# Cross attention of the samples: score and value products take the four sequences of a half in turn

## What is computed

```python
def _cross_attend(h, mk, mv, p):
    n, t = h.shape[:2]                                  # samples: n = 8, t = 4
    q = (h @ p['w_xq']).reshape(n, t, XA_HEADS, XA_HEAD_DIM)
    logits = jnp.einsum('nthd,nmhd->nhtm', q, mk).astype(jnp.float32) * XA_HEAD_DIM ** -0.5
    pr = jax.nn.softmax(logits, axis=-1).astype(mv.dtype)
    o = jnp.einsum('nhtm,nmhd->nthd', pr, mv).reshape(n, t, D_MODEL)
    return o @ p['w_xo']
```

## Time and profile before

| | |
|---|---|
| median of 3 runs | 1905.02 us (1904.67 to 1906.63) |
| profiled execution's own time | 1907.62 us |
| its span, first to last instruction | 1905.6 us |
| PE busy | 1817.0 us, 95% |
| DVE busy | 925.2 us, 49% |
| ACT busy | 530.8 us, 28% |
| mean granted TensorE clock | 0.979 |
| `cross_sample`, first score pass to first pass of the next block | 953.6 to 1009.5 us |

### The profile page before, as it was taken

One profiled execution on the slowest core, in us unless ns is written; L12 is line 12 of the kernel. 1 busy time (PEld: TensorE's weight loads), 2 busy tenths in 40 slices (PEclk: granted clock), 3 DMA queues, 4 the chain that ended last, 5 costly groups with the idle time before them and its releaser, 6 DMA issues. The chain is left out here.

```text
span 1905.6 us, 28207 instructions
## 1 busy us (share of the span) xinstructions
PE 1817.0 (95%) x11818; PEld 1613.5 (85%) x11818; DVE 925.2 (49%) x1881; ACT 530.8 (28%) x1089; POOL 249.9 (13%) x110
## 2 busy tenths in 40 slices
PE   8999988589999899999989999999999999999997
PEld 6889977357767769998935679999999999999997
DVE  6422130467787754433411336545544545455547
ACT  7421000258888522201301212111102101111121
POOL 0011200000000000000000104223224213313320
PEclk9999999789999999999999999999999999999999
DMA  5122657611120341113070012011011101101102
GB/s 192 39 87 56 189 156 195 192 67 57 57 80 14 114 147 50 34 45 133 1 309 22 0 39 77 4 64 67 23 45 67 37 31 67 56 12 67 56 16 91
DMA packets 98306, 145.57 MB, mean 76 GB/s; under 512 B 40637, under 2 KB 73597, under 8 KB 96541
## 3 DMA queue, kind: packets, MB, share of 16 engines
q1 hardware_dynamic: 94094, 140.62, 22.1%
q10 hardware_dynamic: 4088, 3.17, 0.6%
HBM read 132.69 MB, written 14.19 MB: 77 GB/s over the span
## 5 line engine op out<-in xcount | busy, mean ns | idle before, releaser
L1928 PE MATMUL ps<-ff_in_high,ff_weights_low 128*128 128x352 f32 x1056 | 342.6, 324 | 0.0
L1928 PE MATMUL ps<-ff_in_high,ff_weights_high 128*128 128x352 f32 x1056 | 340.2, 322 | 0.0
L1928 PE MATMUL ps<-ff_in_low,ff_weights_high 128*128 128x352 f32 x1056 | 338.0, 320 | 0.0
L1928 PEld LDWEIGHTS ps<-ff_in_high,ff_weights_high 128*128 128x128 f32 x1056 | 198.8, 188 | 0.3
L1928 PEld LDWEIGHTS ps<-ff_in_low,ff_weights_high 128*128 128x128 f32 x1056 | 198.3, 188 | 0.2
L1928 PEld LDWEIGHTS ps<-ff_in_high,ff_weights_low 128*128 128x128 f32 x1056 | 198.1, 188 | 0.0
L2132 DVE TENSOR_TENSOR x<-ps,x 128x352 f32<-128x352 f32 x216 | 113.3, 525 | 134.5 <-PE ps L1946 134.5
L1897 POOL TENSOR_TENSOR ff_weights_low<-ff_weights,ff_weights_high 128x1024 fp32r<-128x1024 f32 x44 | 106.0, 2409 | 456.3 <-ACT ff_weights_high L2028 456.3
L1946 PE MATMUL ps<-ff_act_high,ff_down_high 128*128 128x352 f32 (+1 forms) x496 | 158.3, 319 | 0.2
L1946 PE MATMUL ps<-ff_act_high,ff_down_low 128*128 128x352 f32 (+1 forms) x496 | 156.6, 316 | 0.0
L1946 PE MATMUL ps<-ff_act_low,ff_down_high 128*128 128x352 f32 (+1 forms) x496 | 156.5, 316 | 0.0
(11 more groups left out here) (335 smaller groups left out, 3508.3 us busy)
## 6 DMA issues: line engine op xcount, KB each, us to landing
ff_weights<-in_w_up SPq DMA_DIRECT2D x22, 512.0 KB, 4.5
ff_weights<-in_w_gate SPq DMA_DIRECT2D x22, 512.0 KB, 4.4
ff_down<-in_w_down SPq DMA_DIRECT2D x22, 512.0 KB, 3.5
top<-in_mem_v SPq DMA_DIRECT2D x8, 1024.0 KB, 16.5
top<-in_mem_kt SPq DMA_DIRECT2D x6, 1024.0 KB, 10.1
x<-in_xt SPq DMA_DIRECT2D x3, 1408.0 KB, 10.1
x<-in_pool_cmp SPq DMA_DIRECT2D x32, 128.0 KB, 3.1
big<-in_pool_cmp SPq DMA_DIRECT2D x32, 128.0 KB, 2.7
```

The costliest lines, as they stand in the source:

```text
L1928: last = nc.tensor.matmul(K.bank[3 * s + x][:, 0:b - a], wt[:, s, ws], h[:, k, a:b], start=k + n == 0, stop=k == KD - 1 and n == 2)
```

## The change

Both loops of products are turned inside out, for scores and for values: the sequence `x` is now the innermost loop. The scores run over the eight pieces `c` and in each over the four sequences; the values over the output bank `b` and the piece `m`, and in each over the four sequences. Number, shapes, operands and sums of the products stay. The waits for keys and for values stand in the first round of four (each ahead of its sequence's first product), and the semaphores `k_used` and `pv` are raised in the last round, once for each sequence.

```diff
-                for x in range(4):
-                    n = 4 * half + x
-                    pe.wait_ge(k_came[n], 16)
-                    for c in range(KD):
+                for c in range(KD):
+                    for x in range(4):
+                        n = 4 * half + x
+                        if c == 0:
+                            pe.wait_ge(k_came[n], 16)
                         last = nc.tensor.matmul(K.bank[0][32 * x:32 * x + 32, 0:MEM], qbd[:, c, n, :], kr[n][:, c, :],
                                                 start=c == 0, stop=c == KD - 1)
-                    last.then_inc(k_used, 1)
+                        if c == KD - 1:
+                            last.then_inc(k_used, 1)
...
-                for x in range(4):
-                    n = 4 * half + x
-                    pe.wait_ge(v_came[n], 16)
-                    for b in range(2):
-                        for m in range(2):
+                for b in range(2):
+                    for m in range(2):
+                        for x in range(4):
+                            n = 4 * half + x
+                            if b + m == 0:
+                                pe.wait_ge(v_came[n], 16)
                             last = nc.tensor.matmul(K.bank[2 + b][32 * x:32 * x + 32, :], pt[:, m, 32 * x:32 * x + 32],
                                                     vr[n][:, m, b * 512:(b + 1) * 512], start=m == 0, stop=m == 1)
-                    last.then_inc(pv, 1)
+                            if b + m == 2:
+                                last.then_inc(pv, 1)
```

## The result

| | before | after |
|---|---|---|
| median, four runs each | 1905.18 us (1904.67 to 1906.63) | 1887.61 us (1883.85 to 1890.65) |
| ratio | | 0.9906, 95% interval 0.9883 to 0.9928 |
| span of the profiled execution | 1905.6 us | 1881.8 us |
| `cross_sample`, first score pass to first pass of the next block | 55.9 us | 36.3 us |

The account below looks back on a forecast made before the run. PE's one stream of matmuls was taken to bound the kernel. Faster batches save 26.2 us, 8.5 us of it become waits for loads, so 17.7 us off the 1905.0 us median gives 1887.3 us; range 1883.0 to 1892.0 us.

Parts of the forecast that it names:

- A round of four costs one pass: Score and value products: four strips in turn take one pass's time, 0.216 us at 256 columns; scores 3.6 us a half.
- The landing of values 7 sets the end: Second half's values: ready by 979.1 us but waiting for values 7 until 982.8 us; next block at 991.8 us.
- The waits: PE in `cross_sample`: waits of 2.4 us for values 3, 2.4 us for keys 7, 3.7 us for values 7.
- The values' size: Value batch of each half: 5.3 us instead of 10.53 us; 3.6 us at full clock, 7.0 us at 1.2 GHz throughout.
- The sum: Whole stage: 26.2 us saved on PE, 8.5 us become waits for loads, next block 17.7 us earlier.
- rival 1: Loads in `cross_sample` bind less: 1883.6 us, 1881.9 us with full clock too, 1878.8 us if none mattered; chance 0.12.

Follow-up runs that it names:

- half-load kernel: Changed kernel with half of every load of cached keys and values left out, products as many and as long: 1874.55 us, ratio 0.9820 to before.
- second series: The changed kernel run once more, unaltered, beside the kernel before: 1884.15 us, ratio 0.9889; its profile shows a stage of 38.2 us.
- early keys: Changed kernel with the loads of keys 4, 6 and 7 issued in the block before: 1882.71 us, ratio 0.9883 to the kernel before.

## Why the prediction was right

- **A round of four costs one pass**: right. 3.66 us for 64 passes, 3.6 us forecast, for the width of 256 columns that no row of before had shown. The rule of the Trainium skill, "TensorE: Matmul & The Clock Gate", Part 3, that weight loads overlap only across row groups, is not what this shows: the 64 weight loads of 0.11 us, 7 us of them, lie within the same 3.66 us.
- **The landing of values 7 sets the end**: right, and the step that mattered. It was put at 29.2 us after the stage's start and came at 28.9 us, though issued 5.4 us earlier relative to that start. Reckoned by PE alone, the forecast would have been 1878.8 us, outside the interval of what was measured.
- **The waits**: the three that were named are the three in the trace. Values 3 came a little earlier (8.6 us after the stage's start instead of 8.9), keys 7 too (18.6 instead of 19.0 us). No wait for `w_xo` appeared: its first piece landed 6 us ahead of the next block. How long each landing keeps a ready batch, forecast as 2.4, 2.4 and 3.7 us (8.5 us), came out as 2.0, 1.1 and 3.7 us (6.8 us) in the first profile and 1.9, 4.0 and 2.2 us (8.1 us) in the second, where keys 6 were late too. The parts move with the clock of the batch ahead; only the last landing, which none of them moves, sets the end.
- **The values' size**: mis-sized. 10.53 to 5.3 us was forecast, 5.2 us less, with the half clock as it stood in the trace of before. At full clock the batch takes 3.6 us, and which of the two occurs changes from profile to profile. The two ends were given as bounds; the value chosen, 5.3 us, came about true for the last batch in one of two profiles (5.53 us for its 26 passes; 3.62 us in the other). With no landing waited for, the stage lost 29.1 us, not 26.2, because the value batches of before met the half clock and those of the half-load kernel did not.
- **The sum** of 17.7 us met the median of 17.6 us partly by luck: the second series of the changed kernel is 22.1 us under the kernel before beside it (1884.15 and 1906.22 us), a value that the prediction had for rival 1, and the start of the stage alone scatters by 5 us. What is sure is the stage: 38.2 us forecast, 36.3 and 38.2 us found. The 38.2 us are met to the tenth only because a landing 0.3 us early and a batch 0.2 us longer cancel. The forecast also left the next block's start at half clock; both profiles of the changed kernel start it at full clock, 1.7 us more of gain.

## What to carry to other kernels

When matmuls fill only a strip of the array's columns, put those of different strips next to each other in the program, innermost; it costs no instruction, and here it brought 11.47 us of scores to 6.27 us with two strips in turn and to 3.66 us with four. Before counting the gain, list the landing of every load that the slow batch had hidden: PE meets the latest of a group at its first round, and here the last landing plus the last batch was the new length of the stage. Then move those loads forward: early values 2 and 3 and keys 4 took 8 to 10 us more off the stage. Judge such a stage by its own length in the trace, since the rest of a long program can scatter by as much as the gain in question, here by 5 us.

## What the runs showed of the hardware

- Passes on different column strips need not stand in turn to overlap: each change from one sequence to the next already hid 0.8 us before, with passes of both starting in turn (986.05 to 986.69 us in the trace of before).
- Issuing a load took longer when many full ones were issued close together: values 6 and 7 of the changed kernel, the ninth and tenth load within 7 us, took 0.67 and 4.38 us of SP's time, and values 7 took 0.37 us before. With three loads fewer in the stage (early keys) none of values 4 to 7 took more than 0.47 us, and with all ten at half size none more than 0.60 us. It cost nothing here, as nothing behind it was due. Line L1590, window 954.9 to 962, values 6 and 7:

```profile
L1590 SPq DMA_DIRECT2D top<-in_mem_v x2: 667/2526/4384, 954.2 to 954.9; - x2
```

- With the same program the half clock falls on other batches from profile to profile. In the two profiles of the changed kernel the 26 passes of the first value batch took 6.58 and 3.62 us, the second scores 4.7 and 9.3 us with their waits, and the last 26 value passes 3.62 and 5.53 us. The granted clock of the first of these, in each profile:

```profile
957.50:963.50 6.00, 6.00 (x26) 1.33 (x26) 0.00 (x0) 0.00 (x0) 0.00 (x0) 0.50 1.00 416
...
957.50:961.20 3.70, 3.62 (x26) 0.90 (x26) 0.01 (x1) 0.00 (x0) 0.00 (x0) 1.00 1.01 423
```
